# Channel mixer, seam between its halves: down weights split ahead of the second activation, second tile's products ahead of three norms

## The reference, cut to what matters

```
def conv_ffn(h, buf, w_up, conv_w, conv_b, w_down):
    gate, up = jnp.split(h @ w_up, 2, axis=-1)
    gpad = jnp.concatenate([buf.astype(gate.dtype), gate], axis=1)
    g = causal_dwconv(gpad, conv_w, conv_b)
    return (jax.nn.silu(g) * up) @ w_down, gpad[:, -(FFN_CONV - 1):]
...
    x = x + f
...
    y_prompt = rmsnorm(y_prompt, final_norm_w)
```

## Time and profile before

| | us |
|---|---|
| median of 3 runs | 3143.28 |
| lowest, highest run | 3141.46, 3145.89 |
| the profiled execution | 3141.42 |
| its span, first to last instruction | 3139.6 |

### The profile page before, as it was taken

How to read it: one execution, slowest core, us unless ns; L and a number is a source line. 1 busy time by engine, 2 the same in 40 slices (tenths; PEclk the granted TensorE clock), 3 DMA queues, 4 the chain that set the end, 5 groups by cost and what they waited for, 6 DMA issues and landing times. The chain is left out here.

```text
span 3139.6 us, 45308 instructions
## 1 busy us (share of the span) xinstructions
PE 2982.2 (95%) x16451; PEld 2555.8 (81%) x16451; DVE 1611.2 (51%) x3001; ACT 870.9 (28%) x1670; POOL 748.2 (24%) x512
## 2 busy tenths in 40 slices
PE   8999999989999899869979999999999999999997
PEld 5888889867676699857769999999997788888886
DVE  5113210267687588846645555545556544444445
ACT  4223321223332356533332111122214111111112
POOL 4002100134443254522201221111222211122210
PEclk9999999989999899989989999999999999999999
DMA  4455335567674343348651111111113311111101
GB/s 145 171 201 181 113 135 160 145 183 207 196 217 128 105 124 104 79 126 260 196 221 69 40 40 40 50 71 40 40 54 121 135 54 40 40 48 60 54 14 55
DMA packets 237378, 350.26 MB, mean 112 GB/s; under 512 B 75334, under 2 KB 172135, under 8 KB 231256
## 3 DMA queue, kind: packets, MB, share of 16 engines
q1 hardware_dynamic: 236289, 325.80, 33.4%
q0 software_dynamic: 944, 22.61, 1.9%
HBM read 283.53 MB, written 93.97 MB: 120 GB/s over the span
## 5 line engine op out<-in xcount | busy, mean ns | idle before, releaser
L2631 POOL TENSOR_TENSOR cm_dn_lo<-cm_dn_raw,cm_dn_hi 128x1024 fp32r<-128x1024 f32 x44 | 108.3, 2484 | 974.3 <-ACT cm_dn_hi L2680 974.3
L3368 PE MATMUL pj_acc<-pj_w_hi,pj_h_hi 128*128 128x480 f32 (+3 forms) x896 | 334.3, 373 | 0.9 <-DVE pj_h_lo L3243 0.9
L3369 PE MATMUL pj_acc<-pj_w_lo,pj_h_hi 128*128 128x480 f32 (+3 forms) x896 | 332.6, 371 | 0.0
L3370 PE MATMUL pj_acc<-pj_w_hi,pj_h_lo 128*128 128x480 f32 (+3 forms) x896 | 332.5, 371 | 0.0
L2924 PE MATMUL cm_g_ps<-cm_h_hi,cm_up_hi 128*128 128x344 f32 (+1 forms) x880 | 310.2, 352 | 11.2 <-DVE cm_h_lo L2736 10.9
L2926 PE MATMUL cm_g_ps<-cm_h_hi,cm_up_lo 128*128 128x344 f32 (+1 forms) x880 | 308.8, 351 | 0.0
L2924 PE MATMUL cm_u_ps<-cm_h_hi,cm_up_hi 128*128 128x344 f32 (+1 forms) x880 | 308.2, 350 | 0.0
L2925 PE MATMUL cm_g_ps<-cm_h_lo,cm_up_hi 128*128 128x344 f32 (+1 forms) x880 | 308.0, 350 | 0.0
L2926 PE MATMUL cm_u_ps<-cm_h_hi,cm_up_lo 128*128 128x344 f32 (+1 forms) x880 | 307.8, 350 | 0.0
L2925 PE MATMUL cm_u_ps<-cm_h_lo,cm_up_hi 128*128 128x344 f32 (+1 forms) x880 | 307.0, 349 | 0.0
L3249 DVE TENSOR_TENSOR pj_w_lo<-area,pj_w_hi 128x480 fp32r<-128x480 f32 (+3 forms) x112 | 75.6, 698 | 380.8 <-ACT pj_w_hi L3205 380.8
(11 more groups left out here) (451 smaller groups left out, 6467.7 us busy)
## 6 DMA issues: line engine op xcount, KB each, us to landing
area<-in_w_up SPq DMA_DIRECT2D x44, 1024.0 KB, 7.2
fp_kv_low<-in_fox_kv SPq DMA_DIRECT2D x168, 256.0 KB, 3.0
area<-in_fox_kv SPq DMA_DIRECT2D x88, 256.0 KB, 3.0
cm_dn_raw<-in_w_down SPq DMA_DIRECT2D x44, 512.0 KB
out_s_win<-in_cache POOLq DMA_DIRECT2D x8, 2047.0 KB, 9.8
proj_a<-area SPq DMA_DIRECT2D x48, 240.0 KB
sp_raw<-proj_b SPq DMA_DIRECT2D x16, 640.0 KB, 4.0
area<-in_w_a SPq DMA_DIRECT2D x10, 960.0 KB, 7.5
```

The costliest lines, as they stand in the source:

```text
L2631: pool.tensor_tensor(dn_lo[:, s], dn_raw[:, s], dn_hi[:, s].bitcast(F32), ALU.subtract).then_inc(dn_ready, 1)
L3368: pe.matmul(out, h_hi[:, k, place(t)], w_hi[:, j % 2, k, 0:wide], start=(k == 0), stop=False)
L3369: pe.matmul(out, h_hi[:, k, place(t)], w_lo[:, j % 2, k, 0:wide], start=False, stop=False)
L3370: last = pe.matmul(out, h_lo[:, k, place(t)], w_hi[:, j % 2, k, 0:wide], start=False, stop=(k == KT - 1))
```

## The change

It touches the order on two engines at the seam and splits helpers so that the order can be written.

On ScalarE, `gates` becomes `copy_gates` (the copies from `g_ps`) and `activate` (the Silu). `split_down(second, 0)` now stands between the two for s = 1, where it stood behind both. On VectorE, the products of s = 0, block 0 come ahead of norms 0 and 1 and those of block 1 behind them, where both blocks came behind; norms 2 and 3, which stood between `convolve(second, 0, 1)` and `multiply(second, 0, 1)`, now come behind the latter, together with norm 4.

```
@@ ScalarE, the seam
-            gates(second, 0, (0,))
+            copy_gates(second, 0, 0)
+            activate(second, 0, 0)
             squares(first)
-            gates(second, 0, (1,))
+            copy_gates(second, 0, 1)
             split_down(second, 0)
+            activate(second, 0, 1)
             split_up(second, 1)
@@ VectorE
-            def multiply(H, i, s):
+            def multiply(H, i, s, blocks=None):
...
-                for b in range(nb):
+                for b in blocks or range(nb):
@@ VectorE, the seam
             convolve(second, 0, 0)
             scale_of(first, 0)
+            multiply(second, 0, 0, (0,))
             normed(0), normed(1)
-            multiply(second, 0, 0)
+            multiply(second, 0, 0, (1,))
             convolve(second, 0, 1)
-            normed(2), normed(3)
             multiply(second, 0, 1)
-            normed(4)
+            for n in range(2, 5):
+                normed(n)
             for n in range(second.yt):
                 add(second, 0, n)
```

More of the change, by code:

```diff
@@ L2660, in split_up, with copy_gates, activate, gates @@
                 split_up_of(H, i, 1)
-            def gates(H, i, parts=(0, 1)):
+            def copy_gates(H, i, s):
                 nb, at = H.nb, H.at
-                for s in parts:
-                    n0 = (i * 2 + s) * nb
-                    for b in range(nb):
[L2667 to L2674, removed]
+                n0 = (i * 2 + s) * nb
+                for b in range(nb):
+                    act.wait_ge(gated, H.blocks0 + n0 + b + 1)
+                    act.wait_ge(prod_ready, H.two0 + n0 + nb)
+                    act.activation(gate[:, s, HALO + at[b]:HALO + at[b + 1]], g_ps[:, b, 0:H.widths[b]], ACT.Copy
+                                   ).then_inc(gate_ready, 1)
+            def activate(H, i, s):
+                nb, at = H.nb, H.at
+                n0 = (i * 2 + s) * nb
+                for b in range(nb):
+                    act.wait_ge(conv_ready, H.two0 + n0 + 2 * nb + b + 1)
+                    act.activation(gate[:, s, at[b]:at[b + 1]], conv[:, 0:H.widths[b]], ACT.Silu
+                                   ).then_inc(act_ready, 1)
+            def gates(H, i):
+                for s in range(2):
+                    copy_gates(H, i, s)
+                    activate(H, i, s)
             def split_down(H, i):
```

## The result

| | before | changed |
|---|---|---|
| median us (7 runs each) | 3142.39 | 3150.78 |
| lowest, highest | 3135.83, 3148.95 | 3147.42, 3154.75 |
| ratio to before, 95% interval | | 1.0023 [1.0013, 1.0033] |
| span of the profiled run | 3139.6 | 3149.0 |

The change makes the kernel slower, by 8.4 us in the medians and by 7.2 (4.1 to 10.4) in the ratio. The forecast was 3147.2, +3.9. So the first question is how much of it belongs to the seam.

A forecast was written before the change was run, and what follows sets the result against it. TensorE, busy 95% of the span, was taken as the bound. Its later start on tile 2, behind a late load, gave +3.9 us; added to the median 3143.28, this made 3147.2, range 3141.5 to 3152.

The forecast's parts named there:

- the seam: Between the kernel's halves: two TensorE stops and slow clock behind them, holding 12.6 us in all, 0.4% of the span.
- ScalarE: At s=1: `dn_hi` starts at 2408.6, not 2421.16, and `dn_lo` at 2409.8, 12.5 us earlier, at no cost to ScalarE.
- VectorE, start: Products of block 0 and norms 0 and 1: `a_lo` and norm 0 each meet a `dn_lo`; norm 1 ends at 2417.4.
- TensorE, up projection: Second half's trip 0: block 1's products come late, so TensorE starts 0.4 us late and ends at 2425.0.
- VectorE, middle: Products of s=1 and norms 2 to 4: each `up_lo` holds one operation; norm 2 ends at 2437.7.
- both rivals on this: Norms 2 to 4: norms not held by GpSimd, +2.0 us, chance 0.07; norm 2 ahead of waiting `up_lo`, −0.5, 0.09.
- SyncE: Tile 0's load, queued behind the store awaiting norm 2, lands at 2442.9, 4.8 us after issue; `add` 0 waits for it.
- The sum: TensorE resumes tile 2 at 2444.2, not 2440.35: +3.9 us, 3145.3 for a run like the profiled one.
- safe afterwards: Additions behind tile 0: tile 1's load delays `add` 1 to 2446.6, needed only at 2449; the others have 2 us or more.
- The clock: TensorE behind the longer stop: half clock for the next 5 us, the same 2.8 us loss; bounds −1.4 to +0.5.
- slower by over 0.2%: Whole kernel slower by more than about 6.3 us: chance 0.12, from the drawn-out load and 0.03 of the forecast's tail.
- The drawn-out load: Rival: neighbouring stores and loads delay tile 0's load, which lands near 2448.0; +9.0 us, 3152.3; chance 0.09.

The follow-up runs named there:

- a7: Changed kernel, with ScalarE splitting the up weights of trip 1 only when all nine norms are done: seam 52.0 us, median 3138.41 us, ratio 0.9977.
- a6: Changed kernel, with SyncE issuing the load of tile 0 ahead of the store of tile 2: seam 57.9 us, median 3143.95 us, ratio 1.0001.
- the twin: Changed kernel's text with before's order put back on both engines, run twice: seams 56.7 and 57.2 us, ratios 0.9998 and 1.0001.
- a8: Before's order, with trip 1's up weights split only when all nine norms are done: seam 48.6 us, median 3137.55 us, ratio 0.9970.
- a1: Changed kernel's text with before's order put back on both engines: seam 56.7 us, median 3143.11 us, ratio 0.9998.
- a9: Changed kernel's text with before's order on both engines, timed a second time: seam 57.2 us, median 3147.12 us, ratio 1.0001.
- a11: Changed kernel, norm 2 ahead of the products of s=1 and trip 1's up weights split behind the nine norms: seam 49.8 us, ratio 0.9981.
- a4: Changed kernel with norm 2 alone put back ahead of the products of s=1: seam 57.1 us, median 3146.87 us, ratio 1.0011.

## Why the prediction was right, point by point

- *ScalarE.* `dn_hi` was to start right behind the copies, and `dn_lo` 1.2 us later: 2413.69 and 2414.92, as said.
- *VectorE, start.* `a_lo` held to 2412.8, norm 0 to 2416.2, norm 1 to 2417.4: in before's time (5.1 us less, here and below) it was 2412.8, 2416.1 and 2417.3. Both turns were as said.
- *TensorE, up projection.* It was to go on 0.4 us late and end at 2425.0: it went on 0.3 late and ended at 2425.0.
- *VectorE, middle.* Tile 0's products start at 2426.2: 2426.2. `a_lo` and norm 2 each held by one `up_lo`: 4.98 and 5.5 us; norm 2 ends at 2437.7: 2437.6. So a norm does wait, and the waiting GpSimd instruction goes ahead of the norm that comes back to back; both rivals on this fall, by this row and by a7, where the hold on `up_lo` shortened both.
- *SyncE.* Landing 4.8 us behind the issue, at 2442.9: 4.9 us, at 2442.9. `add` 0 waited 3.0 us for it. a6 shows that this wait alone is worth 3.1 us at tile 2, and 3.3 to 4.2 in the seam. The least that I measured for this load was 3.7, in a6 with one store beside it. The Trainium skill's 3.2 us (estimate from "DMA: Bandwidth & Descriptors", section "Anatomy of one DMA — SWDGE (gpsimd) path") is short of every one of them, and the sum by it, +2.3, would have been short too. But that section gives its figures for transfers on GpSimd's path, and this load is issued by SyncE, so these runs don't test the page: the prediction held a neighbouring figure against its term.
- *The sum.* Tile 2 at 2444.2 (+3.9): 2444.25 (+3.9). The seam was +4.3 in the profile; over all three profiles of either order it was +3.4 to +5.4. What I called safe afterwards was not quite: `add` 6 waited 2.5 us for its load (6.3 us to its landing), as all loads now follow in 18 us where they had 30, and TensorE's trip 1 stood 0.3 us for it; I had worked the landings out to tile 1 only.
- *The clock.* Taken as unchanged behind the longer stop: 0.50 for about 6 us both times.
- *The total.* Forecast +3.9, measured +7.2 (4.1 to 10.4). What fell short is what was put at nothing, a difference outside the seam: 5.1 of the profiled pair's 9.4 us lie ahead of it, and a spread of runs as large arises there in one kernel. So the seam was called rightly (+3.9, measured +4.3), while the total came out at about twice the forecast for a reason that I can't give, and that it still lies within my range I owe to the room that I left for the spread. I gave "slower by over 0.2%" only 0.12, and the ratio's centre lies just there (0.23%). I had taken the spread from three runs (4.4 us); 35 runs show 16 to 20.
- *The drawn-out load*, my rival for a slower kernel, would give nearly the same total (3152.3), but not this trace: there its load lands 10 us behind its issue, and it landed after 4.9.

## What to carry to other kernels

When an instruction is moved in a list written by hand, follow what it releases on the DMA queue as well: a norm moved by 16 us took a store with it, and behind the store, in the same queue, the load that the next addition needed. When an operation of VectorE is several times its usual length, look at GpSimd's timeline at the same time before reordering VectorE: two of the four stretched operations were worth more than any order that I tried. One wait that holds the GpSimd work beside them, which ended 22 us before it was needed, gave 8 to 9 us. And where totals of like runs differ by 10 us, measure a change of 4 by a stretch between two rows that lie on either side of it.

## What the runs showed that I had not expected

- A stop of TensorE of 3.7 to 3.8 us was followed by half clock in before, and by full clock in a8. The 6 us behind the second stop had a mean clock of 0.50, 0.72 and 0.62 in before, a1 and a9, and from the start of tile 2 to the gate copy it took 25.0, 23.9 and 24.4 us: by this, seams of one order differ by some 1 us.
- The time from issue to landing of tile 0's 512 KB load was 3.7 to 4.2 us with one store beside it (a6, a11, a4), and 4.8 to 5.0 where a store and a load were also issued within 1.3 us behind it (before, the twin, the changed kernel, a7). It was 6.3 and 7.1 for the last two loads of the changed kernel.
- In the seams above, where a GpSimd instruction waited while VectorE ended an operation, it went first, and VectorE then got one of the stretched kinds in before GpSimd's next: beside the two `up_lo` of the changed kernel `a_lo` took 4.98 us and norm 2 5.51, one each, and the norm behind them 1.27.
